# Hybrid decoder layer on one core: memory keys turned during the heads, parked in DRAM and read back as slabs

## The reference

```python
def mem_kv(mem, g_mem, w_xk, w_xv):
    m = rms_norm(mem, g_mem)
    mk = einsum('bmd,de->bme', m, w_xk)      # (B, 256, 4, 512)
    mv = einsum('bmd,de->bme', m, w_xv)
    return mk, mv

def cross_attend(h, w_xq, mem_k, mem_v, w_xo):
    q = einsum('btd,de->bte', h, w_xq)       # 4 heads of 512
    s = einsum('bthd,bmhd->bhtm', q, mem_k) * 512 ** -0.5
    p = softmax(s, axis=-1)
    o = einsum('bhtm,bmhd->bthd', p, mem_v)
    return einsum('bte,ed->btd', o, w_xo)
```

## Time and profile before

| | |
|---|---|
| Median of 3 runs | 2720.12 us (2718.7 to 2720.48) |
| Profiled execution | 2720.43 us, span 2718.9 us |
| TensorE | busy 2677.2 us (98%) |
| VectorE | busy 1604.5 us (59%) |
| ScalarE | busy 1064.8 us (39%) |
| GpSimd | busy 237.2 us (9%) |
| DMA | 458.72 MB, mean 169 GB/s |
| Mean granted TensorE clock | 0.994 |

### The profile page before, as it was taken

How to read it: one execution, slowest core, us unless ns; L and a number is a source line. 1 busy time by engine, 2 the same in 40 slices (tenths; PEclk the granted TensorE clock), 3 DMA queues, 4 the chain that set the end, 5 groups by cost and what they waited for, 6 DMA issues and landing times.

```text
span 2718.9 us, 49344 instructions
## 1 busy us (share of the span) xinstructions
PE 2677.2 (98%) x20086; PEld 2553.9 (94%) x20086; DVE 1604.5 (59%) x2387; ACT 1064.8 (39%) x1339; POOL 237.2 (9%) x337
## 2 busy tenths in 40 slices
PE   8999999999999999999999999999999999999998
PEld 7999887899999999999989969999999999999998
DVE  5564564476777767777546334495655555563333
ACT  4333454444444444444334234343323223243233
POOL 0102311011111111111100000001100000010000
PEclk9999999999999999999999999999999999999999
DMA  9746656765555555555564694546655555555555
GB/s 259 215 127 153 219 174 205 233 195 150 154 151 157 156 150 157 149 158 157 133 201 125 215 391 121 145 125 172 160 154 148 145 154 146 143 142 151 149 148 162
DMA packets 694726, 458.72 MB, mean 169 GB/s; under 512 B 14268, under 2 KB 662044, under 8 KB 688492
## 3 DMA queue, kind: packets, MB, share of 16 engines
q1 hardware_dynamic: 680860, 413.32, 53.9%
q0 software_dynamic: 9936, 28.48, 4.0%
q10 hardware_dynamic: 3792, 14.88, 1.5%
HBM read 429.91 MB, written 26.72 MB: 168 GB/s over the span
## 4 chain that ended last, share of the span: by engine, by line
PE 93%; DVE 3%; DMA 2%; ACT 1%; issue 1%; POOL 0%; POOLq 0%; DVEq 0%; SPq 0%; ACTq 0%
PE psum L607 20%; PE psum L612 20%; PE psum L609 20%; PE psum L863 4%; PE psum L1297 4%; PE psum L1295 4%; PE psum L1296 4%; PE psum L868 2%; PE psum L1005 1%; PE psum L1008 1%; PE psum L1001 1%; PE psum L1176 1%; PE psum L721 1%; PE psum L1017 1%; DMA ring<-in_w_in 1%
## 5 line engine op out<-in xcount | busy, mean ns | idle before, releaser
L607 PE MATMUL psum<-x_high,w_high 128*128 128x320 f32 x3808 | 1123.9, 311 | 0.7 <-ACT w_high L2064 0.5
L609 PE MATMUL psum<-h_low,w_high 128*128 128x320 f32 x3312 | 974.3, 309 | 0.0
L1349 DVE TENSOR_TENSOR w_low<-ring,w_high 128x2048 fp32r<-128x2048 f32 x292 | 675.7, 2314 | 310.9 <-ACT w_high L2064 310.4
L2064 ACT ACTIVATE w_high<-ring 128x2048 fp32r<-128x2048 f32 x294 | 561.7, 1911 | 672.5 <-PE psum L612 545.6
L607 PEld LDWEIGHTS psum<-x_high,w_high 128*128 128x128 f32 x3808 | 713.2, 188 | 6.3 <-issue 2.4
L609 PEld LDWEIGHTS psum<-h_low,w_high 128*128 128x128 f32 x3312 | 622.0, 188 | 1.6
L612 PE MATMUL psum<-x_high,w_low 128*128 128x320 f32 x3808 | 597.4, 309 | 0.0
L612 PEld LDWEIGHTS psum<-x_high,w_low 128*128 128x128 f32 x3808 | 568.5, 188 | 0.0
L1295 PE MATMUL psum<-y_high,w_down_high 128*128 128x320 f32 x704 | 218.2, 310 | 1.2 <-DVE w_low L1968 1.2
L1297 PE MATMUL psum<-y_high,w_low 128*128 128x320 f32 x704 | 218.4, 310 | 0.0
L1296 PE MATMUL psum<-y_low,w_down_high 128*128 128x320 f32 x704 | 216.7, 308 | 0.0
(11 more groups left out here) (433 smaller groups left out, 2910.0 us busy)
## 6 DMA issues: line engine op xcount, KB each, us to landing
ring<-in_w_in SPq DMA_DIRECT2D x128, 1024.0 KB, 5.8
ring<-in_w_up SPq DMA_DIRECT2D x88, 1024.0 KB, 5.7
ring<-in_w_down SPq DMA_DIRECT2D x64, 704.0 KB, 4.8
ring<-in_w_xk SPq DMA_DIRECT2D x16, 1024.0 KB, 5.7
ring<-in_w_xv SPq DMA_DIRECT2D x16, 1024.0 KB, 5.1
ring<-in_w_out SPq DMA_DIRECT2D x16, 1024.0 KB, 6.1
ring<-in_w_xq SPq DMA_DIRECT2D x16, 1024.0 KB, 6.1
ring<-in_w_xo SPq DMA_DIRECT2D x16, 1024.0 KB, 6.1
```

The source lines that it names most:

```text
L607: mm(out, w_hi[:, j % 2, k, :], x_hi[:, k, :], start=k == 0, stop=False)
L609: mm(out, w_hi[:, j % 2, k, :], lo[:, k, :], start=False, stop=False)
L1349: V.tensor_tensor(w_lo[:, j], ring[:, j], w_hi[:, j % 2].bitcast(FP32), ALU.subtract).then_inc(N.slab_lo, 1)
L2064: F(w_hi[:, j % 2], ring[:, j], ACT.Copy).then_inc(N.slab_hi, 1)
```

## The change

A new buffer in DRAM, `kt_dram`, holds the keys of 9 items turned within 32 x 32 blocks: for each item 8 groups of 32 memory tokens, each [128 partitions, 16 chunks x 32 tokens].

- In the heads, pass `it` of the loop treats sample `it` (k = 0 to 7, 32 memory tokens each) and a ninth piece (k = 8) of 32 tokens of the prompt's keys. SP loads a piece by four DMAs, one for each group of 32 partitions, in runs of 32 floats (128 B), into one of two buffers of 128 x 512 (`keys_load`); VectorE turns it in place, as 32 x 32 blocks (`keys_turned`); SP stores it (`keys_store`).
- In SP's list, behind slab n: the store of piece n - 4 (from n = 4), which waits for VectorE's turn of that piece, then the load of piece n - 3 (from n = 3). Behind slab 11 the store of piece 8 follows as well, ahead of the next pass's slab 12. The load of `s_old` keeps its place behind g = 4, after these.
- In VectorE's list, the turn of piece 6e + g - 1 stands behind low(g), for g = 1 to 6 of the first head and g = 1 to 3 of the second.
- Before `w_xq` SP loads the keys of items 0, 1 and 3; item 2 goes into the room of `xT` after 8 slabs of `w_xq`, once POOL has parked `xT` in DRAM. POOL fetches it back after the second slab of `w_xo`. Items 4 to 8 follow from the end of the queries on.
- In the attention `chunk_T` and its copies are gone. Scores read the key tile itself, as 8 runs of 32 columns 512 apart. The turning of the samples' probabilities stands behind the last prompt score.
- Two slabs of `w_xo` are issued behind the fifth value tile and two behind the eighth, where four stood ahead of the third key tile.

```diff
+            def keys_store(it, k):
+                dst = kt_dram[ds(it, 1), :, k].rearrange("o p x -> (o p) x") if k < 8 else \
+                    kt_dram[DB][:, ds(it, 1)].rearrange("p o x -> p (o x)")
+                sp.wait_ge(N.kt_turned, it * 9 + k + 1)
+                sp.dma_start(dst, kt_buf[k % 2]).then_inc(N.memo_sent, 16)
+
+            def keys_load(it, k):
+
+                sp.wait_ge(N.memo_sent, it * 144 + 128 + 16 * max(k - 1, 0))
+                for i in range(4):
+                    if k < 8:
+                        src = A["cache_mem_k"][0][ds(it, 1), 32 * k:32 * k + 32].rearrange("o m h d -> (o m) (h d)")
+                    else:
+                        src = O["new_mem_k_prompt"][0, 0][ds(it * 32, 32)].rearrange("m h d -> m (h d)")
+                    sp.dma_start(kt_buf[k % 2][32 * i:32 * i + 32].rearrange("p (c d) -> p c d", d=32),
+                                 src.rearrange("m (c i d) -> i m c d", i=4, d=32)[i]).then_inc(N.kt_loaded, 16)
+
             with sp.Fori(0, NHG // 2) as it:
                 for e in range(2):
                     for g, col in enumerate((O_HF, O_HQ, O_HI, O_HG, O_GA, O_GB)):
                         n = 6 * e + g
                         slab(it * 12 + B_HG + n, n % R, w_in[:, :, ds(it * (2 * P) + col + e * P, P)])
+                        if n >= 4:
+                            keys_store(it, n - 4)
+                        if n >= 3:
+                            keys_load(it, n - 3)
+                        if n == 11:
+                            keys_store(it, 8)
                         if g == 4:
                             sp.wait_ge(N.head_done, two_back(it, 2, e))
                             sp.dma_start(s_old[:, e], hg_in[ds(it * 2 + e, 1)].rearrange("o c b v -> (o c) b v"))\
@@ -537,35 +566,50 @@
             stretch(B_OUT, 16, A["w_out"][0].rearrange("(k p) n -> p k n", p=P), 0)
             sp.wait_ge(N.head_done, NHG)
             sp.wait_ge(N.state_sent, 32 * NHG)
-            for n in range(2):
-                sp.dma_start(kx[:, n], mem_k[n]).then_inc(kx_loaded[n], 16)
-            stretch(B_XQ, 16, A["w_xq"][0].rearrange("(k p) n -> p k n", p=P), 0)
-            def kx_load(i, src):
-                slot, _ = kx_item(i)
-                sp.dma_start(kx_slot[slot], src).then_inc(kx_loaded[slot], 16)
+            sp.wait_ge(N.memo_sent, 128 + 16 * 9 * (NHG // 2))
+
+            def keys_in(i):
+                place, loaded, _ = KEYS[i]
+                sp.dma_start(place, kt_dram[i].rearrange("p g x -> p (g x)")).then_inc(loaded, 16)
+
+            keys_in(0)
+            keys_in(1)
+            k3 = kt_dram[3].rearrange("p g (c m) -> p g c m", m=32)
+            sp.dma_start(k3_most.rearrange("p g c m -> p g (c m)"), k3[:, :, 0:12].rearrange("p g c m -> p g (c m)"))\
+              .then_inc(in_K3, 16)
+            sp.dma_start(k3_rest.rearrange("p g c m -> p g (c m)"), k3[:, :, 12:16].rearrange("p g c m -> p g (c m)"))\
+              .then_inc(in_K3, 16)
+            w_xq = A["w_xq"][0].rearrange("(k p) n -> p k n", p=P)
+            stretch(B_XQ, 8, w_xq, 0)
+            sp.wait_ge(N.x_parked, 16)
+            keys_in(2)
+            stretch(B_XQ + 8, 8, w_xq, 8 * P)
 
             w_xo = A["w_xo"][0].rearrange("(k p) n -> p k n", p=P)
-            for j in range(R):
+
+            def values_in(b, wait, count):
+                place, loaded, _ = VALUES[b]
+                sp.wait_ge(wait, count)
+                sp.dma_start(place.rearrange("p (m d) -> p m d", m=2), mem_v[b]).then_inc(loaded, 16)
+
+            sp.wait_ge(N.slab_used, B_XQ + KD)
+            keys_in(4)
+            keys_in(5)
+            for i, used in ((6, 0), (7, 1), (8, 2)):
+                sp.wait_ge(N.sx_mm, XD * (used + 1))
+                keys_in(i)
+            values_in(0, N.sx_mm, XD * 6)
+            values_in(1, N.sx_mm, XD * 7)
+            values_in(2, N.sx_mm, XD * 8)
+            sp.dma_start(new_values, new_mv).then_inc(in_D, 16)
+            values_in(3, N.sx_mm, XD * 8)
+            values_in(4, N.sx_mm, XD * 9)
+            for j in range(2):
                 slab(B_XO + j, j, w_xo[:, :, j * P:(j + 1) * P])
-            sp.wait_ge(N.slab_used, B_XQ + KD)
-            kx_load(2, mem_k[2])
-            for b in range(3, DB):
-                sp.wait_ge(N.kx_T, XD * (b - 2))
-                kx_load(b, mem_k[b])
-            sp.wait_ge(N.kx_T, XD * 6)
-            sp.wait_ge(N.memo_sent, 16 * 8)
-            kx_load(DB, new_mk)
-            sp.wait_ge(N.kx_T, XD * 7)
-            kx_load(DB + 1, new_mv)
-            for b in (0, 2, 1, 3, 4, 5, 6, 7):
-                if b < 2:
-                    sp.wait_ge(N.kx_T, XD * (8 + b))
-                elif b == 2:
-                    sp.wait_ge(N.sx_mm, XD * DB)
-                elif b > 3:
-                    sp.wait_ge(N.vx_mm, V_AT[b - 4 if b < 7 else 4])
-                slot, _ = V_ITEM[b]
-                sp.dma_start(kx_slot[slot], mem_v[b]).then_inc(kx_loaded[slot], 16)
+            for b in range(5, DB):
+                values_in(b, N.vx_mm, V_AT[b - 4])
+            for j in range(2, R):
+                slab(B_XO + j, j, w_xo[:, :, j * P:(j + 1) * P])
...
-            def chunk_T(c):
-                i, dt = c // XD, c % XD
-                slot, loaded = kx_item(i)
-                if dt == 0:
-                    pe.wait_ge(kx_loaded[slot], loaded)
-                if c >= 3:
-                    pe.wait_ge(N.kx_edve, chunk_before(c))
-                    pe.wait_ge(N.kx_eact, chunk_before(c))
-                for x in range(XH):
-                    for mt in range(2):
-                        at = (x % 2) * MEM + mt * P
-                        last = tr(bank(chunk_bank(c) + x // 2)[:, at:at + P],
-                                  kx_slot[slot][:, mt, x * 512 + dt * P:x * 512 + (dt + 1) * P], ident)
-                last.then_inc(N.kx_T, 1)
-
             def chunk_scores(c):
                 b, dt = c // XD, c % XD
-                pe.wait_ge(N.kx_edve, c + 1)
-                pe.wait_ge(N.kx_eact, c + 1)
+                if dt == 0:
+                    pe.wait_ge(KEYS[b][1], KEYS[b][2])
                 if b < DB:
                     g, e = b // 4, b % 4
                     for x in range(XH):
-                        last = mm(bank(g)[32 * x:32 * x + 32, 0:MEM], qm[:, g, 4 * x + dt, 32 * e:32 * e + 32],
-                                  kxT[:, c % 3, x], start=e == 0 and dt == 0, stop=e == 3 and dt == XD - 1,
-                                  skip_group_check=True)
+                        last = mm(bank(g)[32 * x:32 * x + 32, 0:MEM].rearrange("p (g m) -> p g m", m=32),
+                                  qm[:, g, 4 * x + dt, 32 * e:32 * e + 32], keys_of(b, 4 * x + dt),
+                                  start=e == 0 and dt == 0, stop=e == 3 and dt == XD - 1, skip_group_check=True)
                 else:
                     for qt in range(2):
                         for x in range(XH):
-                            last = mm(bank(4 + 2 * qt + x // 2)[:, (x % 2) * MEM:(x % 2 + 1) * MEM],
-                                      qx[:, 4 * x + dt, qt * P:(qt + 1) * P], kxT[:, c % 3, x],
+                            last = mm(bank(4 + 2 * qt + x // 2)[:, (x % 2) * MEM:(x % 2 + 1) * MEM]
+                                      .rearrange("p (g m) -> p g m", m=32),
+                                      qx[:, 4 * x + dt, qt * P:(qt + 1) * P], keys_of(b, 4 * x + dt),
                                       start=dt == 0 and x % 2 == 0, stop=dt == XD - 1, skip_group_check=True)
                 last.then_inc(N.sx_mm, 1)
 
-            chunk_T(0)
-            chunk_T(1)
             pe.wait_ge(N.qm_ready, DB)
-            for c in range(0, XD * DB - 2, 2):
-                chunk_T(c + 2)
-                chunk_T(c + 3)
+            for c in range(K_CHUNKS):
                 chunk_scores(c)
-                chunk_scores(c + 1)
-            for c in range(XD * DB - 2, K_CHUNKS):
-                if c + 2 < K_CHUNKS:
-                    chunk_T(c + 2)
-                chunk_scores(c)
-                if c == XD * DB + 1:
-                    pe.wait_ge(N.sx_prob, 2)
-                    for g in range(2):
-                        for mt in range(2):
-                            last = tr(bank(0)[:, (2 * g + mt) * P:(2 * g + mt + 1) * P], px[:, g, mt * P:(mt + 1) * P], ident)
-                    last.then_inc(N.px_T, 1)
+            pe.wait_ge(N.sx_prob, 2)
+            for g in range(2):
+                for mt in range(2):
+                    last = tr(bank(0)[:, (2 * g + mt) * P:(2 * g + mt + 1) * P], px[:, g, mt * P:(mt + 1) * P], ident)
+            last.then_inc(N.px_T, 1)
 
...
-                low(1)
+                def keys_turned(k):
+
+                    dve.wait_ge(N.kt_loaded, it * 576 + 64 * (k + 1))
+                    V.transpose(kt_buf[k % 2], kt_buf[k % 2]).then_inc(N.kt_turned, 1)
+
+                def low_and_keys(g):
+                    low(g)
```

(64 more changed lines are left out.)

37 lines of the change are left out of this document (20 added, 17 removed).

## The result

Four runs of the changed kernel have a median of 2762.12 us (2758.56 to 2765.4); the kernel before, run beside it, 2719.43. The ratio is 1.0157, with a 95% interval of 1.0145 to 1.0169: **42.7 us slower**, where 17.6 were forecast. The sign was right and 2762 lies in the range, but the size was off by more than a factor of two.

The account below looks back on a forecast made before the run. TensorE was taken to pace the heads, turning keys and fetching tiles to bound the attention. The sum: 2720.4 + 27.2 lost in second heads - 9.5 gained in the attention = 2738 us, range 2719 to 2768.

Parts of the forecast that it names:

- Rival 2: Second heads: slab 12, the next pass's first, is in time and only the attention's gain stands; 2711 us, chance 0.12.
- rival 5: Attention: keys still arrive one by one, values end at 1644, only the loss is left; 2747 us, chance 0.06.
- Rival 4: Heads: DMA is the bound, a 128 B run costing a 512 B row's time, 96 of 97 us; 2771, chance 0.14.
- rival 1: The forecast itself, SP's queue in second heads: 2723 to 2750 us, likeliest 2738, chance 0.58.
- at full clock: Two heads in the middle of the loop: TensorE busy 97.00 of 97 us at full clock, setting the pace.
- the chain of the second head: Second heads: slabs behind stores that wait for turns make slab 12's tile 3.4 us late; 27 us over eight passes.
- In first heads this hides: First heads: slab 5 and later go out 8 to 12 us later, landing at or just after their split, unfelt by TensorE.
- eight passes: Second heads: the 3.4 us of lateness counted for eight passes, 27 us lost.
- high end of 56: Heads: 3.8 us for a piece and 1.04 us for a turn, about 7 us a pass, 56 us lost.
- 3.1 us of all engines per piece: DMA in the heads: nine pieces cost 9 x (2.4 + 0.7) = 28 us, making 83 of 97 us.
- The term of 14 tiles at 5.36 us each: Attention: tiles DMA must bring behind the last query tile, at 391 GB/s, 75.1 us.
- The price of the two `w_xo` slabs: Attention: two slabs ahead of the last three value tiles, 3.8 us of all engines each, 7.6 us.

Follow-up runs that it names:

- e8: Kernel of e5 with the stores back in their old places in SP's list, third buffer kept: 2765.58 us, 1.0167.
- e5: Changed kernel with all stores of pieces one slab later and a third buffer, counts per buffer: 2709.73 us, 0.9963.
- e2: Changed kernel with pieces loaded in whole 2 KB rows in place of 128 B runs: 2755.84 us, 1.0136.
- e3: Changed kernel with VectorE's turns of pieces replaced by a write of one column: 2757.93 us, 1.0138.
- e7: Kernel of e6 with loads of whole 2 KB rows in place of 128 B runs: 2709.05 us, 0.9964.
- e6: Kernel of e5, first pass's first piece waiting only for the previous stage's last attention evacuation, not the memory outputs: 2710.19 us, 0.9969.
- e4: Changed kernel with only the ninth store moved, behind the next pass's first slab: 2737.74 us, 1.0071.
- e10: Kernel of e5 with the two w_xo slabs behind the last three value tiles, not ahead: 2717.67 us, 0.9997.
- e1: Changed kernel without loading, turning or storing pieces; the attention reads key slabs from the caches as they lie: 2708.04 us, 0.9957.

## Why the prediction was wrong in size

**The path was right.** SP's queue is what costs: e8 against e5 changes the place of the stores alone, for 56 us, and e2, e3 and e7 take short runs and turns away for 6, 4 and 1. Rival 2 (slab 12 in time) and rival 5 (no gain in the attention) did not happen. Rival 4 fell twice over: the share was 0.77 and not 96 of 97 us, and e5 runs at 0.82 with one slab late, by 1.1 us. But 2762 lies above the 2723 to 2750 of rival 1 as well: 57.2 us were lost where 27.2 stood in the sum. Of the 30 us that are missing, 18.5 are the first step below and 11.5 the other two.

**The step that failed first** is one that the sum does not have. It charged a late tile with its lateness alone and left TensorE, which it had read "at full clock", at full clock behind the stall; that the clock might fall was put at nothing, without a reason. In the changed kernel it falls to the lower level ten times in the heads, and TensorE's matmuls take 18.5 us longer. At the start of each of these stretches TensorE had just been idle or still was, for 1.9 to 4.3 us. In the head shown:

```profile
972.45:1020.92 48.47, 48.47 (x460) 46.99 (x459) 36.16 (x61) 21.99 (x31) 6.33 (x4) 1.00 0.53 144
1002.32:1057.48 55.16, 50.28 (x460) 48.50 (x459) 38.48 (x65) 22.23 (x31) 5.59 (x4) 0.97 0.81 200
```

The head is 6.7 us longer, 4.9 of them idle and 1.8 in the same 460 matmuls. The fourteen heads between the first and the last together lose 28.5 us idle and 11.8 in matmuls, the last head 4.5 and 5.3. Not every stall comes with a low stretch: the second head of pass 1 has none, with idle times of 1.83 and 2.77 us. What decides it, no run here shows.

**The step that failed next** is the chain of the second head, where I took four loads and a store "at 0.57 us each". Set against the rows, in before's times (measured less 29.87):

| | predicted | measured |
|---|---|---|
| piece 5 turned | 975.4 | 975.4 |
| slab 10 issued | 978.35 | 979.25 |
| level products start | 988.9 | 989.9 |
| level products done | 995.75 | 996.8 |
| piece 8 turned | 998.7 | 999.6 |
| slab 12 issued | 999.35 | 1000.8 |
| slab 12 split | 1007.0 | 1008.6 |
| its tile starts, against 1003.59 | 3.4 late | 5.1 late |

From the store's issue to the slab's it is 1009.12 - 1005.40 = 3.72 us, not 2.85. The 0.57 of the earlier trace rows was the distance from a slab's issue, itself 0.37 us long, to the next; a load's issue is longer. Source lines of the loads and of the slabs, from 600 to 1300 us (count, ns min/median/max, starts):

```profile
L548 SPq DMA_DIRECT2D arena<-in_cache_mem_k x216: 563/573/4433, 600.6 to 1295.2; - x108
```

```profile
L510 SPq DMA_DIRECT2D ring<-in_w_in x82: 377/416/3789, 604.3 to 1296.0; - x82
```

With the gaps between them four loads take 2.86 us, one every (2.86 - 0.57) / 3 = 0.76. The Trainium skill (Perfetto Trace Analysis, DMA Instruction — HWDGE (DVE, Sync)) says that the issuing engine is held until all descriptors are generated. If these were as many as the runs, a load (512) should be cheaper to issue than a slab (2048); the rows show 0.57 against 0.42 us, so the count of runs alone doesn't give it.

This 0.9 us goes through the whole chain unchanged, and at store 8 another 0.6 comes, where SP needs 1.04 us from the store to the slab. The turn was well priced, 0.70 us for 0.65, and the order of the chain was right. The seven second heads are idle for 28.5 us, 4.1 each in place of 3.4.

**The third step** is one of placement, in two places. "In first heads this hides" is right for seven of eight (3.0 us in all) but not for the first pass, 7.1 us. There slab 5, 10.5 us late, meets POOL's fetch of x (under e6), and I had looked at no row of it. And I took "eight passes" alike; the last head, where the late slab is `w_out`'s first, lost 9.8. 8 x 3.4 = 27.2 stands against 37.3 + 7.1 + 3.0 + 9.8 = 57.2. That my high end of 56 was reached, and 2762 lies in the range, is luck: that end stood for dear runs and turns, and neither was dear.

**The split of the second head's loss.** I gave 1.1 of 3.4 us to slab 10 and the rest, 2.3 a pass or 18 us, to the ninth store. e4 gave 24 back: the seven second heads lose 21.8 of their 37.3 us less, 58% where my split has 68%, and the last head 7.4 less.

**DMA in the heads.** I took 3.1 us of all engines per piece. e5 has (0.82 - 0.57) x 97 / 9 = 2.7. The Trainium skill's rule of 512 B (DMA: Bandwidth & Descriptors, Specifications) points the right way: by e7 the short runs take 1.1 us of all engines more per piece. They don't take the 3.8 us that I drew from it, and no run here shows a read-modify-write.

**Attention.** The term of 14 tiles at 5.36 us each is too large. In the trace after the change keys land 4.90 us apart (1615.38, 1620.27, 1625.16, 1630.07), 428 GB/s, and values 5.0. It is not that they come faster than before: in the trace before, tiles land 4.97 us apart too where nothing lies between them (1560.76 to 1580.66). The 391 GB/s was the mean of a window in which other tiles landed up to 6.8 us apart, and I took it for the rate of a tile. The last tile landed 80.1 us after the queries' end, where I had it at 84.6, and the gain was 13.9 us and not 9.5, inside the 5 to 14.5 of the estimate. The price of the two `w_xo` slabs was about right, 6.8 us for 7.6 (they land at 1663.57 and 1666.83 behind a tile at 1660.00), but it could not be taken back: with them behind the last three tiles, e10 is 8 us slower.

**Still open**: what decides whether the clock falls behind a stall. And second heads of one kernel differ: those of e4 lose from nothing to 4.3 us. The two dearest (4.3 and 3.7) are the two with a stretch at the lower clock; why their idle times differ, 1.7 to 2.9 us, was not taken apart.

## What to carry to other kernels

When a job with a wait is put into a queue that also feeds the bottleneck, what counts is the position of the wait, not the job: here 18.9 MB of loads, 72 turns and as much in stores were nearly free (3.3 us), and the same work one slot earlier cost 57. Ask of each wait in such a list whether what it waits for is done when the queue gets there, and if it isn't, put it behind the next urgent item or have the producer do it first; one swap on VectorE and one moved store gave back 41 of the 43 us. Don't price a late tile by its lateness alone: here 57.2 us of loss were 38.7 us of waiting and 18.5 us of matmuls at the lower clock around these waits. Walk the first and the last pass by themselves, and count the spacing of DMA issues from rows of that kind of DMA, not from their durations alone.

## What the runs showed of the hardware that was not expected

In the changed kernel stalls of TensorE of 1.9 to 4.3 us came with stretches at the lower level of its clock, most of them 3.4 us long, in which a matmul of 128x320 took up to 0.61 us in place of 0.31; the kernel before has one such stretch in its heads. An issue on SP, 0.4 us for a slab, took 7.34 us when the DMA share was 1.05. A DMA share of 0.82 over a whole pass, with 9 x 2048 short runs in it, made no slab late in e5 (ScalarE waited for one, 1.1 us), though slabs now took 6.4 us to land in place of 5.7 (medians). Key and value tiles came at 417 GB/s over 56 us, 428 between two keys. And in the profile of e1 the granted clock reads 0.95 through the heads where the kernel before has 1.00, both near the higher level of 2.4 GHz, while each head is only 0.1 us of 48.5 longer: this reading, some hundredths lower, hardly showed in the time there.
